# Loading the second expert projection by whole 4 KB rows in place of 2 KB column halves

## What is computed

```python
def _moe_swiglu(h, w_router, b_router, w_exp_in, w_exp_out):
    logits = (h @ w_router).astype(jnp.float32) + b_router
    top_val, top_idx = lax.top_k(logits, TOP_K_EXPERTS)
    top_w = jax.nn.softmax(top_val, axis=-1)
    ...
    for e in range(N_EXPERTS):
        out = out + combine[..., e:e + 1] * _swiglu(h, w_exp_in[e], w_exp_out[e])
```

## Time and profile before

| | |
|---|---|
| median of three runs | 1663.64 us |
| profiled execution, device time | 1659.23 us |
| its span, first to last instruction | 1657.3 us |
| TensorE busy | 1498.7 us, 90% |
| VectorE busy | 869.6 us, 52% |
| ScalarE busy | 656.8 us, 40% |
| mean granted TensorE clock | 0.951 of full |
| DMA packets, bytes | 303225, 333.99 MB |
| expert stage, first matmul to the last pass's store | 1228 to 1614 us |

### The profile page before, as it was taken

How to read it: one execution, slowest core, us unless ns; L and a number is a source line. 1 busy time by engine, 2 the same in 40 slices (tenths; PEclk the granted TensorE clock), 3 DMA queues, 4 the chain that set the end, 5 groups by cost and what they waited for, 6 DMA issues and landing times.

```text
span 1657.3 us, 22153 instructions
## 1 busy us (share of the span) xinstructions
PE 1498.7 (90%) x8359; PEld 1181.3 (71%) x8359; DVE 869.6 (52%) x1281; ACT 656.8 (40%) x903; POOL 40.2 (2%) x65
## 2 busy tenths in 40 slices
PE   5999999999989999989399999999749999999993
PEld 4666766666689999876166666667638888888872
DVE  2101856664354443331014857642358888898964
ACT  1221115433233332222011144431347877888752
POOL 0000000000000000000001000000020000000010
PEclk8999999999989999999699999999769999999996
DMA  8755633224447887864933332124539999999962
GB/s 274 213 155 182 203 105 108 74 69 131 139 140 229 239 240 242 239 187 123 321 77 102 107 125 90 51 90 152 190 124 333 382 383 384 384 383 386 385 250 68
DMA packets 303225, 333.99 MB, mean 202 GB/s; under 512 B 32288, under 2 KB 219112, under 8 KB 303144
## 3 DMA queue, kind: packets, MB, share of 16 engines
q1 hardware_dynamic: 283874, 308.52, 57.3%
q10 hardware_dynamic: 17798, 19.11, 3.4%
q0 software_dynamic: 1472, 5.24, 0.9%
HBM read 311.37 MB, written 21.46 MB: 201 GB/s over the span
## 4 chain that ended last, share of the span: by engine, by line
PE 81%; DMA 5%; DVE 4%; ACTq 3%; ACT 3%; SPq 2%; issue 1%; POOL 1%; POOLq 0%; DVEq 0%
PE mmp L725 38%; PE mmp L1083 7%; PE mmp L1085 7%; PE mmp L1084 7%; PE mmp L1001 3%; PE mmp L1003 3%; PE mmp L1002 3%; DMA ring<-in_w_ffn_out_dram 2%; SPq L493 2%; PE py L701 1%; PE py L761 1%; DMA ring<-in_w_ffn_in_dram 1%; ACTq L1302 1%; PE px L701 1%; ACTq L1298 1%
## 5 line engine op out<-in xcount | busy, mean ns | idle before, releaser
L725 PE MATMUL mmp<-hT,ring 128*128 128x320 f32 (+1 forms) x1760 | 493.6, 440 | 15.8 <-ACT hT L1214 7.9
L725 PEld LDWEIGHTS mmp<-hT,ring 128*128 128x128 f32 (+1 forms) x1760 | 335.0, 193 | 157.0 <-issue 14.9
L1240 ACT ACTIVATE tmp<-mmp 128x320 f32<-128x320 f32 x70 | 30.6, 438 | 348.4 <-PE mmp L725 249.3
L1707 DVE SCALAR_TENSOR_TENSOR conv<-u_conf,dwc,conv 128x350 f32<-128x350 f32 x240 | 124.7, 578 | 1.7
L1001 PE MATMUL mmp<-h_hi,wd_hi 128*128 128x320 f32 x352 | 111.7, 317 | 9.7 <-DVE h_lo L1816 9.3
L1792 DVE TENSOR_TENSOR wd_lo<-ring,wd_hi 128x2048 fp32r<-128x2048 f32 (+1 forms) x38 | 76.4, 2010 | 76.4 <-ACT wd_hi L1418 76.1
L1002 PE MATMUL mmp<-h_lo,wd_hi 128*128 128x320 f32 x352 | 110.0, 312 | 0.0
L1003 PE MATMUL mmp<-h_hi,wd_lo 128*128 128x320 f32 x352 | 109.9, 312 | 0.0
L1913 DVE TENSOR_TENSOR more_lo<-more,we_hi_a 128x2048 fp32r<-128x2048 f32 (+1 forms) x48 | 92.2, 1935 | 26.4 <-ACT we_hi_a L1469 25.4
L1083 PE MATMUL mmp<-we_hi_a,xg_hi 128*128 128x512 f32 (+1 forms) x256 | 99.0, 387 | 2.4 <-DVE xg_lo L1918 2.4
L1085 PE MATMUL mmp<-we_hi_a,xg_lo 128*128 128x512 f32 (+1 forms) x256 | 97.2, 380 | 0.0
(11 more groups left out here) (329 smaller groups left out, 2499.7 us busy)
## 6 DMA issues: line engine op xcount, KB each, us to landing
ring<-in_w_in_dram SPq DMA_DIRECT2D x104, 512.0 KB, 4.7
ring<-in_w_ada_dram SPq DMA_DIRECT2D x96, 512.0 KB, 6.5
ring<-in_w_exp_in_dram SPq DMA_DIRECT2D x64, 512.0 KB, 7.8
more<-in_w_exp_in_dram SPq DMA_DIRECT2D x64, 512.0 KB, 11.1
more<-in_w_exp_out_dram SPq DMA_DIRECT2D x48, 512.0 KB
ring<-in_w_ffn_in_dram SPq DMA_DIRECT2D x44, 512.0 KB, 7.1
ring<-in_w_branch_dram SPq DMA_DIRECT2D x48, 256.0 KB, 3.0
more<-in_w_exp_in_dram SPq DMA_DIRECT2D x32, 384.0 KB
```

What stands on the lines that cost most here:

```text
L725: ins = nc.tensor.matmul(mmp[0:m, 2 * (q % 2) + b, 0:T], v[:, i, c0:c0 + m], rhs(i), start=(i == 0), stop=(i == k - 1))
L1707: ins = V.scalar_tensor_tensor(conv[:, c, :], src, tap, conv[:, c, :], ALU.mult, ALU.add)
```

## The change

Only the description of the second projection's transfers changes. Before, both DMAs of a chunk cover all its rows in all 128 partitions, the first with columns 0 to 511 and the second with columns 512 to 1023. After it, a chunk of one row block is loaded as rows 0 to 63 into partitions 0 to 63 and rows 64 to 127 into partitions 64 to 127, and a chunk of two row blocks is loaded one row block at a time (by `halves`); every piece is a whole row of 4 KB. There are two DMAs in a chunk as before, of the same sizes, behind the same waits.

```diff
                             f, f1 = OUT_AT[k - 12], OUT_AT[k - 11]
                             v = we_raw(k)[:, 0:(f1 - f) * D].rearrange("p (k n) -> p k n", k=f1 - f)
                             src = wout_e[:, f:f1, :]
-                            parts = [(v[:, :, h * 512:(h + 1) * 512], src[:, :, h * 512:(h + 1) * 512])
-                                     for h in range(2)]
+                            if f1 - f == 1:
+                                parts = [(v[h * 64:(h + 1) * 64], src[h * 64:(h + 1) * 64]) for h in range(2)]
+                            else:
+                                parts = halves(v, src, f1 - f)
                         for dst, src in parts:
                             sp.dma_start(dst, src).then_inc(e_full[k % MSLOTS], 16)
```

## The result

The changed kernel takes 1716.13 us (median of four runs, 1702.42 to 1725.39) against 1663.56 of before (1660.06 to 1665.3): ratio 1.0312, 95% interval 1.023 to 1.0394. On a second occasion it was 1712.43 against 1662.76, ratio 1.0296 (1.0262 to 1.0331). So it is some 50 us slower, where 24 were forecast. The profiled execution took 1702.42 us, 43.2 more than that of before.

A forecast was written before the change was run, and what follows sets the result against it. TensorE was taken to bound the kernel, DMA engines just below. Net 4.5 us in each of seven passes made 31.6, less 6.1 slack 25.5, rounded to +24: 1688 us from 1663.64, range 1664 to 1700.

The forecast's parts named there:

- net DMA time of a pass: Expert stage: halves' 5.5 us less longer rows' 0.95 gives 4.5 us more DMA time in a pass.
- the step from the profiled execution to the median: Whole kernel: the median of the runs stands 4.4 us above the profiled execution, added to the forecast time.
- What bounds the kernel: Expert stage: TensorE sets the time, with the DMA engines just below it at a demand of 384 GB/s.
- (a) Row length: Second projection's loads: 4 KB pieces for 2 KB take 0.95 us less DMA time in a pass (0 to 1.5).
- (b) Doubles: Three chunks of two row blocks: each transfer still covers 128 partitions, so nothing beyond the gain from row length.
- (c) Halves: Five chunks of one row block: 64-partition transfers at 220 GB/s against 410 cost 5.5 us more in a pass.
- slack: Expert stage: the DMA queue may gain 6.1 us of backlog before TensorE stands still, once over the whole stage.
- a little overlap of opposite halves: Where halved chunks meet full-width ones, some overlap is likely, so the sum of 25.5 us was rounded down to +24.
- R1: Rival: engine couples partly out of step, 1.8 us in a pass, +6.5 us, 1670 us; chance 0.20.
- R2: Rival: conflict costs hidden by longer rows' gain and the slack, time unchanged at 1664 us; chance 0.16.
- R3: Rival: halves cost nothing, the queue drains and matmuls come closer together, 6.5 us at most, 1657 us; chance 0.04.
- R4: Rival: halves at 200 GB/s, net 5.75 us in a pass, +34 us, 1698 us; chance 0.60 together with the forecast.

The follow-up runs named there:

- e9: Kernel before with one of three expert-stage matmuls left out and the subtraction cut to 64 columns, all transfers kept: a pass of 47.50 us.
- e10: Full-width 4 KB rows as in e4, with one of three matmuls left out and the subtraction cut short: a pass of 46.66 us.
- e2: Against the kernel before, only chunks of two row blocks changed to 4 KB rows, a block at a time: 1662.47 us, ratio 0.9998.
- e4: Changed kernel, but each chunk of one row block loaded by one DMA over all 128 partitions, 4 KB rows everywhere: 1662.52 us, ratio 0.9996.
- e3: Against the kernel before, only chunks of one row block changed, to partitions 0 to 63 and then 64 to 127: 1710.58 us, ratio 1.0287.
- e8: Changed kernel, but chunks of one row block split into even and odd rows, 64 partitions each with step 2: 1662.68 us, ratio 0.9992.
- e15: e8 with one of three expert-stage matmuls left out and the subtraction cut short: a pass of 46.67 us.
- e13: e5 with one of three expert-stage matmuls left out and the subtraction cut short: a pass of 50.0 us (49.7 to 50.2).
- e11: Changed kernel with one of three expert-stage matmuls left out and the subtraction cut short: a pass of 52.82 us.
- e1: The changed kernel again, unaltered, on another occasion, against the kernel before: 1712.43 us, ratio 1.0296.
- e12: Changed kernel without the first gather of result rows (1.3 MB), its rows left out of the output: 1702.85 us, ratio 1.0252.
- e5: e4 with chunk 12 alone loaded in two halves of 64 partitions, one row block in a pass: 1680.0 us, ratio 1.0085.
- e16: Changed kernel with the two halves of every second single-block chunk issued in the other order: 1712.99 us, ratio 1.0311.
- e14: e4 with chunks 12 to 14 in halves, one of three matmuls left out and the subtraction cut short: a pass of 53.7 us.

## Why the prediction was right in direction and wrong in size

The forecast was +24 us, the measured loss is 50 to 53. The mechanism was right. What failed are the sizes in the sum: the net DMA time of a pass (4.5 us put, 5.0 to 6.2 found), the last gather (not in the sum, 2 to 3 us), and the step from the profiled execution to the median (4.4 us taken over from the kernel before, 13.7 and 13.1 us found).

*What bounds the kernel.* Right. TensorE without a wait, the DMA side just below. e9 puts a number to it, 0.33 us in a pass.

*(a) Row length.* 0.95 us were forecast, 0.84 measured (e9 to e10), and worth nothing in time (e2, e4). Right.

*(b) Doubles.* Nothing, as forecast (e2).

*(c) Halves.* The mechanism and its place were right: the loss is there with them (e3), gone at full width (e4), and gone when each DMA of 64 partitions reaches both sides of partition 64 (e8, e15). The Trainium skill's rule on the DMA port swizzle (SBUF — State Buffer), by which the ports that the partitions reach set the rate, agrees with e8 as with e3. By its section on hitting both halves two such DMAs give 6% over one; the slow slices of the changed kernel run at 227 to 276 GB/s, neighbours included, against 220 assumed, thus somewhat better; those of e13 run at 196 to 226, not better.

*The mis-sized terms of the sum.* In terms of the profiled execution:

| term | forecast | measured |
|---|---|---|
| halves, in a pass | +5.5 | +6.2 (e11 - e10) |
| longer rows, in a pass | -0.95 | -0.84 (e10 - e9) |
| free DMA time in a pass of before | 0 | -0.33 (e9) |
| net over TensorE's pass | 4.5 | 5.0 (e11), 5.0 to 5.5 in the profile, 5.9 to 6.2 in the second (e1) |
| seven passes | 31.6 | 35 to 43 |
| slack, once | -6.1 | -6 to -7, from the sum |
| last gather in a full queue | not seen | +2 to 3 (e12) |
| stage | +24 | +35.2, +40.2 in the second profile |
| median over profiled execution | 4.4 | 13.7, 13.1 on the second occasion |

The half-rate share carried more bytes than its own: the term took 2.62 MB at 220 GB/s, but from the slices of the steady pass the slow part is some 12 of 40 slices, 16 us at 245 GB/s, 3.9 MB. The error of the step was to take neighbours as undisturbed. The forecast also rounded down for "a little overlap of opposite halves" with full-width chunks; where the two met, both were slowed (e13). A step that was left out altogether is the gather: in the kernel before its 1.3 MB fell into the same full queue and cost nothing (the pass with it takes 47.85 us as the others), which the slack can have held; once the slack is spent, it costs. "What is late next" should have been asked of all users of the queue.

*The slack.* The 6.1 us were read where TensorE uses a chunk; the stop comes earlier, at the hidden rows behind a waiting cast. From the passes of the changed kernel the size still comes out about right: seven passes at 5.2 and a gather of 2 to 3 us make 38.4 to 39.4, the passes were longer by 0 + 2.8 + 5.2 + 5.5 + 5.0 + 5.1 + 8.9 = 32.5, so 5.9 to 6.9 us were held. But in e5 the slack held much less than that, so as a fixed store it is not shown.

*Timed against profiled.* The rest, some 10 us, is in runs whose inside isn't seen. The profiled executions of the changed kernel (1702.4, 1699.4) were the fastest of theirs; the others took 1709 to 1725, at a mean clock of 0.936 to 0.941. Of the kernel before, 19 executions lie between 1658.0 and 1670.6 (0.944 to 0.951), and they too are slower where the mean clock is lower: 1665.0 to 1670.6 for the three at 0.944, 1660.3 and 1660.6 for the two at 0.951. So some of the 10 us may be clock. It can't be all, since the first profiled execution had 0.938 and was still the fastest of its four. In several steady passes above, which have gaps in TensorE's stream, the granted clock is 0.97, but these passes are bound by transfers and no longer than those at 1.00. Whether the timed executions lost the rest to engines that had drifted apart, as in the profile of e16, stays open.

*The rivals.* R1 (engines out of step, half the price) is refuted, and e13 turns it over: the engines are further out of step there than in e11 (a lead of 4.5 to 7.6 us against 2.6 to 3.2), and a block costs more, not less. R2 and R3 fall with the result. R4 (+34) was nearest, partly by luck: its 6.7 us for the halves of a pass are above the 6.2 measured, and it had neither the gather nor the gap between profile and median. The range ended 16 us too low.

*What stays open.* One block in halves costs 3.4 us, three cost 7.0 and five 6.2, and the engines drift apart in the first two and hardly in the third. Why they drift there, and whether the drift makes the price or follows from it, is not shown: the trace has no engine's name on a packet. Nor is it clear why e5's passes (48.9 to 49.3 us) are shorter than those of e13, which has the same transfers and less to compute.

## What to carry to other kernels

When the DMA queue is full, ask of each transfer not only its bytes and its row length but which partitions it writes: two DMAs on partitions 0 to 63 and 64 to 127 brought the rate of their stretch of the queue from 393 down to some 245 GB/s, while the same bytes in one DMA of 128 partitions, or in two by even and odd rows, cost nothing. Where TensorE never waits, a change that helps the transfers gains nothing, and one that hurts them shows as soon as their spare time is used up (0.33 us in 47.8 here). The DMA share does not tell how much that is: it was 1.03 to 1.05 with spare time and without. Find the transfers' own pass by taking work off the other engines before and after. Then price everything else that uses the queue, since it all comes onto the path at once.

## What the runs showed of the hardware that was not expected

- A small dose is dear. One block of 0.52 MB in halves among full-width transfers made the transfers' pass 3.4 us longer (50.03 against 46.66), five made it 6.2 longer.
- DMAs of 64 partitions with a partition step of 2 ran at the full rate (46.67 us in a pass, 393 GB/s), stretches with DMAs of 64 adjacent partitions at 196 to 276 GB/s, and full-width packets among them took twice as long (138 ns in place of 68).
- With halves in the queue the DMA engines can drift apart, by up to 11 us in e14, where full-width transfers keep the lead at 1.8 (e10).
- 4 KB rows in place of 2 KB for a third of the bytes raised the rate of a full queue from 387 to 393 GB/s (e9, e10).
